# Which engine copies the turned cache rows in the merged GLA and gather loop of a hybrid decoder step

## What is computed

```python
# per chunk of tokens: scores with pairwise decays, output, carried state
scores = einsum('bhtd,bhsd,bhtsd->bhts', qc, kc, exp(rel))
o = einsum('bhts,bhse->bhte', scores, vc) + einsum('bhtd,bhde->bhte', qc * exp(bcum), s)
s_new = exp(b_end) * s + einsum('bhsd,bhse->bhde', kc * exp(b_end - bcum), vc)
```

```python
nsa_past = cache_nsa_kv[l][page_table]
hid = einsum('bnrhd,rde->bnhe', r[:, :-1] + pe_lo, w1[:16]) + einsum('bnrhd,rde->bnhe', r[:, 1:] + pe_hi, w1[16:]) + b1
s_sc = einsum('bthgd,bhtnsd->bhgtns', qf, k_sel)
```

## Time and profile before

| | |
|---|---|
| median of three timed runs | 2509.69 us (2509.32 to 2512.29) |
| the profiled execution | 2511.87 us, its span 2510.1 us |
| mean granted clock of PE | 0.851 of full speed |
| busy shares of the span | PE 77%, DVE 42%, ACT 26%, POOL 3% |
| 128x512 copies by ACT (L1519) in the stage | 64, mean 597 ns |
| 128x512 copies by DVE (L1618) in the stage | 32, mean 692 ns |

### The profile page before, as it was taken

How to read it: one execution, slowest core, us unless ns; L and a number is a source line. 1 busy time by engine, 2 the same in 40 slices (tenths; PEclk the granted TensorE clock), 3 DMA queues, 4 the chain that set the end, 5 groups by cost and what they waited for, 6 DMA issues and landing times. The chain is left out here.

```text
span 2510.1 us, 33148 instructions
## 1 busy us (share of the span) xinstructions
PE 1939.2 (77%) x13251; PEld 1795.0 (72%) x13251; DVE 1065.7 (42%) x1853; ACT 649.3 (26%) x1157; POOL 81.0 (3%) x100
## 2 busy tenths in 40 slices
PE   6999941347888868887517663875999999999997
PEld 5999930246677747776416563865999999999997
DVE  5222237326777745553311315124344344344334
ACT  5000013224545533332112112013212222222221
POOL 0000000000000022221000000000000000000000
PEclk7999975757999989997755556997999999999999
DMA  5232241441010044551152012102101100100101
GB/s 186 84 101 84 79 154 51 127 101 26 10 18 2 1 148 176 189 174 55 22 85 112 35 43 76 43 9 84 34 34 47 53 33 33 67 33 33 67 17 68
DMA packets 141509, 175.42 MB, mean 70 GB/s; under 512 B 41634, under 2 KB 120026, under 8 KB 138074
## 3 DMA queue, kind: packets, MB, share of 16 engines
q1 hardware_dynamic: 134418, 123.29, 16.6%
q0 software_dynamic: 2304, 33.56, 3.5%
q10 hardware_dynamic: 4688, 17.21, 1.8%
HBM read 135.11 MB, written 43.14 MB: 71 GB/s over the span
## 5 line engine op out<-in xcount | busy, mean ns | idle before, releaser
L58 PE MATMUL ph<-hH,wuH 128*128 128x344 f32 x768 | 246.6, 321 | 37.3 <-DVE wuL L2731 37.3
L58 PE MATMUL ph<-hidH,wdH 128*128 128x344 f32 x768 | 250.2, 326 | 31.6 <-DVE onat L2749 27.2
L2749 DVE TENSOR_TENSOR onat<-ph,onat 128x344 f32<-128x344 f32 x384 | 194.0, 515 | 139.1 <-PE ph L60 138.6
L59 PE MATMUL ph<-hidL,wdH 128*128 128x344 f32 x768 | 247.4, 322 | 0.0
L60 PE MATMUL ph<-hidH,wdL 128*128 128x344 f32 x768 | 247.3, 322 | 0.0
L59 PE MATMUL ph<-hL,wuH 128*128 128x344 f32 x768 | 246.1, 320 | 0.0
L60 PE MATMUL ph<-hH,wuL 128*128 128x344 f32 x768 | 245.9, 320 | 0.0
L58 PE MATMUL pa<-hH,winH 128*128 128x344 f32 (+1 forms) x600 | 194.6, 324 | 3.2 <-DVE winL L317 3.2
L59 PE MATMUL pa<-hL,winH 128*128 128x344 f32 (+1 forms) x600 | 192.2, 320 | 0.0
L60 PE MATMUL pa<-hH,winL 128*128 128x344 f32 (+1 forms) x600 | 192.0, 320 | 0.0
L58 PEld LDWEIGHTS ph<-hidH,wdH 128*128 128x128 f32 x768 | 146.3, 190 | 36.1 <-DVE onat L2749 31.4
(11 more groups left out here) (550 smaller groups left out, 3647.4 us busy)
## 6 DMA issues: line engine op xcount, KB each, us to landing
uact<-in_w_up_dram SPq DMA_DIRECT2D x16, 1024.0 KB, 6.6
hs<-in_w_down_dram SPq DMA_DIRECT2D x16, 1024.0 KB, 4.9
zT_scratch<-z ACTq DMA_DIRECT2D x24, 516.0 KB, 2.7
win<-in_w_in_dram SPq DMA_DIRECT2D x24, 512.0 KB, 3.8
vS_scratch<-page_rows SPq DMA_DIRECT2D x16, 512.0 KB, 4.1
zin<-zT_scratch SPq DMA_DIRECT2D x10, 516.0 KB, 6.9
xT_scratch<-xT ACTq DMA_DIRECT2D x8, 516.0 KB
onat<-xT_scratch SPq DMA_DIRECT2D x2, 2064.0 KB, 7.8
```

What stands on the lines that cost most here:

```text
L58: nc.tensor.matmul(out, wH, mH, start=(k == 0), stop=False)
L59: nc.tensor.matmul(out, wH, mL, start=False, stop=False)
L2749: nc.vector.tensor_tensor(y, ps[4 + n % 4][:, 0:TC], y, ALU.add).then_inc(added, 1)
```

## The change

Four of the twelve copies of a body change their engine, and the change is in every body. The copies of slots 1, 9 and 11 go from DVE to ACT; the copy of slot 2 goes from ACT to DVE. Slots 0, 4, 5, 6, 7, 8 and 10 stay on ACT, and slot 3 on DVE. ACT then makes ten copies of a body where it made eight, and DVE two where it made four. The place of a copy in the order of its engine follows from its slot: on ACT the copy of slot 1 comes after `copy_hidden`, the copy of slot 9 after `sizes`, and the copy of slot 11 after `decays`; on DVE the copy of slot 2 comes after the merge of slot 1.

```diff
         NFILL = 12
-        by_act = (0, 2, 4, 5, 6, 7, 8, 10)
-        by_dve = (1, 3, 9, 11)
+        by_act = (0, 1, 4, 5, 6, 7, 8, 9, 10, 11)
+        by_dve = (2, 3)
```

## The result

The changed kernel takes 2524.62 us in the median of five runs (2521.87 to 2525.62), the kernel before 2510.69 us beside it (2509.32 to 2513.55). The ratio is 1.0051, with a 95% interval of 1.0036 to 1.0065. The forecast was 2508.8 us and "same". The profiled execution of the changed kernel took 2525.62 us.

What follows compares the result with a forecast made beforehand. The prediction took PE to set the merged loop's pace, so only its waits counted; seven borders times 0.13 us gave 0.9 us, and 2509.69 - 0.9 = 2508.8 us, with a range of 2506.7 to 2511.8 us.

Steps and rivals of the forecast that it cites:

- The add: DVE's add of the hidden sums in the merged loop, forecast to start 0.13 us sooner per body without slot 1's copy.
- the stall: PE's idle time before its use of slot 0, forecast to drop from 1.28 to 1.15 us.
- ACT becomes late: Rival: slot 11's copy on ACT passes its use, needing 1.37 us more lateness than worked out; chance 0.01.
- The two clock rivals: Loop clock stops falling in three or more bodies (2497.7 us, 0.04), or also falls at the first stall (2519.9 us, 0.03).
- the first stall: PE's 1.93 us wait before level 1, for DVE's merge of level 0; forecast unchanged, clock staying at 1.00.
- the second: PE's 1.28 us wait before its use of slot 0, for DVE's add; followed by a clock fall costing 1.58 us.
- rows 9: Clock windows around both loop stalls before the change; a different clock in several bodies was to show the prediction wrong.
- relay: Hand-over at the body's border from PE to ACT, DVE's add and PE; forecast 0.13 us shorter, seven times, 0.9 us.
- The rule weighed: By engine loads, DVE busy 56% of the loop is not saturated, so the change brings nothing: 2509.7 us.
- slower: Whole-kernel outcome beyond the bound of about 0.2%, 5.0 us, above the kernel before; chance 0.04.

Runs made afterwards that it cites:

- all_but_slot1: The kernel before with the copies of slots 9 and 11 moved to ACT and slot 2 to DVE, slot 1 left on DVE: 2510.85 us, ratio 0.9998.
- before_late: The kernel before with an idle GpSimd memset of 1490 columns at the start of the mLSTM stage, estimated delay 1.3 us: 2521.98 us, ratio 1.0048.
- after_late: The changed kernel with an idle GpSimd memset of 2430 columns at the start of the mLSTM stage, estimated delay 2.1 us: 2513.81 us, ratio 1.0022.

## Why the prediction was wrong, point by point

- **The step that failed** is in its first paragraph: "an edit inside one stage can change the total only by what it does to that stage's length". The loop's length changed as worked out, and an untouched stage answered with +14.8 us. It failed because the next stage takes over not only the work but also PE's clock and the moment: with the old loop and nothing but an idle operation in front of the scan, 1.3 us gave 2522.0 us and 3.4 us gave 2514.4 us. What the prediction took for a fixed term, the length of the mLSTM scan, lies between 42.4 and 57.3 us in the ten traces of the table, and it never looked at the windows of that scan, where the row of before at 0.50 and 8.80 of 10 us busy gave the warning.
- **The parts of the change** were right. The add moved by 0.13 us, the stall went from 1.28 to 1.16 us (forecast 1.15), the body to 30.63 us, and slots 2, 9 and 11 cost nothing: all_but_slot1 is 0.9998. Slot 11 still has over a microsecond before its use, so "ACT becomes late" did not happen.
- **The two clock rivals** looked at the right mechanism in the wrong place. Both happened, together: behind the fourth border the fall was missing, and in the next bodies the clock fell at the first stall instead of the second. The trace's clock record has six falls in the loop ahead of its tail (three at either stall), and that of before has seven, so the loop lost no time by it. The prediction named such a difference from rows 9 in several bodies as a sign of being wrong, and it came. Windows of after:

```profile
1044.00:1047.00 3.00, 2.00 (x25) 1.67 (x27) 1.61 (x5) 1.52 (x4) 2.76 (x2) 1.00 0.00 0
1047.00:1050.00 3.00, 3.00 (x38) 2.42 (x36) 1.07 (x3) 0.00 (x0) 0.00 (x0) 1.00 0.82 251
1058.00:1060.50 2.50, 0.81 (x9) 0.58 (x8) 2.25 (x7) 0.60 (x1) 1.44 (x1) 1.00 0.49 158
1060.50:1063.90 3.40, 3.40 (x27) 3.18 (x28) 0.77 (x2) 0.00 (x0) 0.00 (x0) 0.51 0.92 304
```

  1047 to 1050 is at 1.00 where rows 9 have 0.53, and 1060.5 to 1063.9 is at 0.51 behind the stall before level 1. The prediction's argument against this, that the place of the first stall relative to its own matmuls is unchanged, was no argument: what moved is its place in time. How 0.13 us could do that is in the same matmuls of four bodies (timeline of after, PE alone; the second figure is how long they took):

```profile
954.43 1.84 PE L1435 MATMUL pr<-hs,w_heads 64*128 64x128 f32 x16 [1.00 <-DVE onat L1624]
985.07 1.76 PE L1435 MATMUL pr<-hs,w_heads 64*128 64x128 f32 x16 [1.00 <-DVE onat L1624]
1015.71 1.68 PE L1435 MATMUL pr<-hs,w_heads 64*128 64x128 f32 x16 [1.00 <-DVE onat L1624]
1046.34 1.16 PE L1435 MATMUL pr<-hs,w_heads 64*128 64x128 f32 x16 [1.00 <-DVE onat L1624]
```

  In the clock record the falls of before are 30.72 us apart, and so are the first three of after, while a body takes 30.76 us before and 30.63 after. So each fall of before comes 0.04 us earlier in its body (the use takes 1.78, 1.82, 1.86 us and so on), each of after 0.09 us later, until the fourth border has none. The traces bear this out in number: of the seven kernels with the old relay six have their seven falls 30.7 us apart (not before_late), of the seven with the shorter relay none has.
- **The rule weighed**, that of the Trainium skill in "Perfetto Trace Analysis", section "Optimizing Scalar/DVE Operations", that moving work off VectorE may make sense if VectorE is saturated, was taken to give 2509.7 us. The three copies that touch no wait of PE fit it, 0.9998; the fourth does not. On the clock, the Trainium skill ties the falls to PE's waits in "TensorE: Matmul & The Clock Gate", section "HAM oscillation — how this bites in real kernels". In the loop the trace agrees in so far as the falls stand at two stalls; in the scan it disagrees: the clock stayed at 0.50 from 1195 to 1225 us in after with PE shown busy 10.00 of 10 us, and in after_late it fell at 1213.0 with no wait over 0.16 us in the ten microseconds before.
- **The chances**: slower had 0.04. The range ended 13 us below the result, since the spread of the runs of one kernel says nothing of a stage whose length hangs on the moment at which it begins.

Open stays what in the scan keeps the clock low, or lets it fall, while PE has no wait, and how the moment acts on it. With the wide matmuls added the clock rose once and stayed up in both traces; none of the scan's own matmuls was changed or taken out.

## What to carry to other kernels

Before you trust a sum that ends at a barrier, read the clock of the stage behind it: where a stage begins at the lower level and PE looks fully busy, its length can depend on when it begins, and a microsecond ahead of it can be worth ten in either direction. To find out, delay the stage by an idle operation of one to three microseconds; if the time does not follow the delay, a measured gain or loss of an edit ahead of it says little about that edit.

## What the runs showed of the hardware

- PE at the 1.2 GHz level, busy 10.00 of 10 us, did not get its clock back for over 30 us (after), and lost it from the upper level with no wait over 0.16 us since it rose (after_late, 1202.8 to 1213.0 us).
- A stall of 1.28 us was followed by a fall of the clock in each of seven bodies (before). With 0.13 us less in that stall, the falls moved to the other stall of the loop after three bodies (after). One fall cost 1.55 us.
- A delay of 1.3 us ahead of the scan of before cost 12 us, one of 3.4 us cost 4 us, and starting 2.0 us sooner cost 12 us.
